# Norm statistics beside the last sums, 512-column projections and written-out layers in a two-block transformer kernel

## The reference

```
def hybrid_layer(x, ...):            # block 1, twice
    h = rmsnorm(x, norm_mix); proj = h @ w_in
    ... fox attention, compressed/selected/window attention, gates ...
    x = x + mixed @ w_out
    h = rmsnorm(x, norm_mlp)
    return x + jnp.square(jax.nn.relu(h @ w_up)) @ w_down
x = rmsnorm(x, norm_final)           # between the blocks
for i in range(2):                   # block 2
    mix = even_mixer(x, ...) if i % 2 == 0 else odd_mixer(x, ...)
    x = layer_norm(ALPHA * x + mix @ w_o[i], ln1_g[i], ln1_b[i])
    ffn = expert_choice_moe(x, ...)
    ple = sigmoid(x @ ple_gate_w[i] + ple_gate_b[i]) * (p[i] @ ple_w[i])
    x = layer_norm(ALPHA * x + ffn + ple, ln2_g[i], ln2_b[i])
# odd_mixer: q, k, v = split(x @ w_in); q = rms_norm(q per head), k = rms_norm(k per head);
# q, k = apply_rope(q), apply_rope(k); softmax(q k^T * HEAD_DIM**-0.5) v
```

## Time and profile before

| | us |
|---|---|
| median of 3 runs | 3708.51 (3707.27 to 3711.32) |
| the profiled execution itself | 3716.81 |
| its span | 3715.0 |
| mean granted clock of TensorE | 0.947 |

### The profile page before, as it was taken

One profiled execution on the slowest core, in us unless ns is written; L12 is line 12 of the kernel. 1 busy time (PEld: TensorE's weight loads), 2 busy tenths in 40 slices (PEclk: granted clock), 3 DMA queues, 4 the chain that ended last, 5 costly groups with the idle time before them and its releaser, 6 DMA issues. The chain is left out here.

```text
span 3715.0 us, 42723 instructions
## 1 busy us (share of the span) xinstructions
PE 3309.8 (89%) x17174; PEld 2279.5 (61%) x17174; DVE 1294.2 (35%) x1709; ACT 976.0 (26%) x1557; POOL 295.7 (8%) x403
## 2 busy tenths in 40 slices
PE   7999899998999999999846779999978787999996
PEld 6875687876876588777744367444437356644442
DVE  4325533333524445242344543111113654311112
ACT  4225333222324414231321431000012343100001
POOL 1004100000102300000000310000000431000000
PEclk9999999999999999999967889999998898999998
DMA  5410233333320114331300124999972101599997
GB/s 155 125 46 1 68 91 91 96 86 82 106 91 23 46 33 137 92 91 34 102 7 15 57 70 160 422 425 424 424 320 78 46 24 58 215 422 424 424 424 290
DMA packets 286517, 587.41 MB, mean 158 GB/s; under 512 B 34666, under 2 KB 228408, under 8 KB 237200
## 3 DMA queue, kind: packets, MB, share of 16 engines
q1 hardware_dynamic: 286352, 585.11, 42.3%
HBM read 581.92 MB, written 2.10 MB: 157 GB/s over the span
## 5 line engine op out<-in xcount | busy, mean ns | idle before, releaser
L2018 PE MATMUL ps<-w_ring,xe 128*64 128x512 f32 x1024 | 234.3, 600 | 6.1 <-PEq L109 5.0
L305 PE MATMUL ps<-h_hi,in_w_hi 128*128 128x512 f32 (+1 forms) x528 | 209.5, 397 | 13.2 <-DVE in_w_lo L353 8.2
L305 PE MATMUL ps<-u_hi,mlp_w_hi 128*128 128x512 f32 x512 | 201.0, 393 | 12.0 <-DVE u_lo L984 12.0
L353 DVE TENSOR_TENSOR mlp_w_lo<-w_ring,mlp_w_hi 128x2048 fp32r<-128x2048 f32 x64 | 146.7, 2292 | 175.8 <-ACT mlp_w_hi L321 175.8
L305 PE MATMUL ps<-h_lo,in_w_hi 128*128 128x512 f32 (+1 forms) x528 | 207.8, 393 | 0.0
L305 PE MATMUL ps<-h_hi,in_w_lo 128*128 128x512 f32 (+1 forms) x528 | 207.5, 393 | 0.0
L305 PE MATMUL ps<-h_hi,mlp_w_hi 128*128 128x512 f32 x512 | 199.4, 389 | 5.6 <-DVE h_lo L367 5.6
L305 PE MATMUL ps<-u_lo,mlp_w_hi 128*128 128x512 f32 x512 | 200.5, 392 | 0.0
L305 PE MATMUL ps<-u_hi,mlp_w_lo 128*128 128x512 f32 x512 | 200.2, 391 | 0.0
L305 PE MATMUL ps<-h_lo,mlp_w_hi 128*128 128x512 f32 x512 | 199.2, 389 | 0.0
L305 PE MATMUL ps<-h_hi,mlp_w_lo 128*128 128x512 f32 x512 | 199.2, 389 | 0.0
(11 more groups left out here) (512 smaller groups left out, 7046.5 us busy)
## 6 DMA issues: line engine op xcount, KB each, us to landing
w_ring<-in_w SPq DMA_DIRECT2D x192, 1024.0 KB, 12.5
ex_front<-in_w SPq DMA_DIRECT2D x96, 1024.0 KB, 13.4
ex_back<-in_w SPq DMA_DIRECT2D x96, 1024.0 KB, 13.4
w_ring<-in_w_in SPq DMA_DIRECT2D x32, 1024.0 KB, 6.6
w_ring<-in_w_up SPq DMA_DIRECT2D x32, 1024.0 KB, 5.7
w_ring<-in_w_down SPq DMA_DIRECT2D x32, 1024.0 KB, 5.6
w_ring<-in_cmp_w SPq DMA_DIRECT2D x16, 512.0 KB, 4.2
w_ring<-in_w_out SPq DMA_DIRECT2D x8, 1024.0 KB, 6.3
```

The lines of the kernel that those rows point to most:

```text
L305: mm = pe.matmul(ps[0:o.rows, k % banks, 0:o.cols], lhsT, rhs, start=(j == 0), stop=(j == len(o.mm) - 1))
L353: dve.tensor_tensor(w.lo[:, n % SPLITS, 0:used], ring.slots[:, n % RING, 0:used], w.hi[:, n % SPLITS, 0:used].bitcast(F32), ALU.subtract). ...
L2018: mm = pe.matmul(ps[rows, bank + half, :], lhsT, slot(2 * m + a)[:, kk, 512 * half:512 * half + 512], start=(k == 0), stop=(k == DC - 1))
```

## The change

- The norm lead loses its norm. `rms_beside` does it beside the last outputs of the gemm before: as soon as DVE has added token tile i's first half of columns, ACT sums its squares; after the second half, ACT sums again and takes the root, and DVE scales the row into ring slots 2 and 3. `first_rows` does the first layer's norm in a stage of its own.
- `residual_tiles` has 4 x 512-column weight tiles; outputs are pieces of 12 matmuls of 512 columns in banks 4c + i that stay open over the tiles of one column half c; only the last is added to x. The MLP's down projection takes this form too; `yT`, `unflip_add` and the fence go, and `needs` waits for the u blocks of one weight tile. With `pairwise` (w_o) the last two token tiles of the second half run whole, 24 matmuls each.
- Layers of block 1 are written out; `wy` prefetches the MLP's first two weight tiles, `mlp` those of the next layer or of `ei`.
- The norm between the blocks is part of the lead of `ei`; x itself is normed by DVE beside four outputs of `ei`.
- `ln1` goes beside `w_o`: bn_stats per half row on DVE, bn_aggr, root on ACT, two passes on DVE per token tile.
- Odd layer: gemm `oi` takes k first and runs on 4 banks; squares on ACT, sums by TensorE as 128-token by 2-head columns (`sq` stationary, 2 columns moving), k's inverse root flipped, spread and multiplied in, q's left out and given to Exp as a scale (and to the maximum by one small multiply) in `gqa`; the halves are swapped by SBUF to SBUF DMA and DVE does the rotation. Stages `on` and `ro` go.
- Names get serial numbers (left out below).

```diff
-    def down(m, n):
-        if m == 0:
-            return to(yT[:, n, :], "A")
-        return dict(v=lambda e, p, st: e.tensor_tensor(yT[:, n, :], yT[:, n, :], p, ALU.add))
-    down_tiles = [[tile(half // P, P, ..., fence=(n == 0)) for n in range(DC)] for m in range(2)]
-    gemm(nc, "mlp", ps, ring, tiles, lead=rms_flips(C, x, I["norm_mlp"][l], h, ring, ...))
-    unflip_add(nc, "da", ps, C, yT, x)
+    down_tiles = [residual_tiles(I["w_down"][l], u, half // P, added(x), m * half, lambda q, m=m: m * (ups + downs) + 4 * q + 3) for m in range(2)]
+    ends = 2 * (ups + downs)
+    tail = rms_beside(C, ring, x, ..., ends - downs // 2 - 4, ends - 4)
+    gemm(nc, "mlp", ps, ring, tiles, 2, nxt, rms_flips(C, I["norm_mlp"][l], h, ring, gain[:, :]), side=tail)
-    gemm(nc, "wy", ps, ring, y_tiles + w_out, 2)
+    tail = rms_beside(C, ring, x, lambda c, i: sgb[:, 4 * c + i, :], n_y + 4, n_y + 12)
+    gemm(nc, "wy", ps, ring, y_tiles + w_out, 2, up_of(I, l, 0)[0:2], side=tail)
-    return [tile(DC, 256, lambda slot, n=n: [(slot, W(w, DC, 256 * n, 256))],
-                 lambda w, n=n: [tm(w, actT, i, 0, 256, range(DC), **add(i, n)) for i in range(TT)]) for n in range(4)]
+    def piece(w, c, i, q, **more):
+        return out(P, 512, [m for j in range(4) for m in products(actT[:, 4 * q + j, i * P:(i + 1) * P], w[:, j, :])],
+                   bank=4 * c + i, first=(q == 0), needs=needs(q) if needs and c == 0 and i == 0 else None, **more)
+    def pieces(w, c, q):
+        if pairwise and c == 1:
+            held.append(w)
+            if q == 0:
+                return [piece(w, c, i, q, final=False) for i in range(2)]
+            rest = [out(P, 512, [...held tiles, 24 products...], bank=4 * c + i, **add(i, c)) for i in (2, 3)]
+            return [piece(w, c, i, q, **add(i, c)) for i in range(2)] + rest
+        return [piece(w, c, i, q, final=(q == quarters - 1), ...) for i in range(TT)]
+    return [tile(4, 512, ..., lambda w, c=c, q=q: pieces(w, c, q)) for c in range(2) for q in range(quarters)]
...
+def rms_beside(C, ring, x, junk, front, back):
+    def square(c, i):
+        def go(act, s):
+            act.wait_ge(s.evac_v, s.done_v[(front if c == 0 else back) + i])
+            act.activation(junk(c, i), x[:, i, 512 * c:512 * c + 512], ACT.Square, accum_out=st[:, SUMS + c, i:i + 1]).then_inc(s.n_squared, 1)
+            if c == 1:
+                act.wait_ge(s.n_squared, TT + i + 1)
+                act.wait_ge(s.n_bias, 1)
+                act.activation(st[:, STD, i:i + 1], st[:, SUMS + 1, i:i + 1], ACT.Sqrt, scale=1.0 / D, bias=st[:, BIAS, i:i + 1]).then_inc(s.n_std, 1)
+        return go
+    def scale(*tokens):
+        def go(dve, s):
+            for i in tokens:
+                dve.wait_ge(s.n_std, i + 1)
+                dve.reciprocal(C.rstd[:, i:i + 1], st[:, STD, i:i + 1]).then_inc(s.n_rstd, 1)
+                dve.wait_ge(s.n_rstd, i + 1)
+                dve.tensor_scalar(rows[:, i, :], x[:, i, :], C.rstd[:, i:i + 1], None, ALU.mult).then_inc(s.n_scaled, 1)
+        return go
+    return beside(..., {back: half, back + 2: scale(0), back + 3: scale(1), back + 4: scale(2, 3)}, nothing)
...
+def layer_norm_beside(nc, ctx, C, x, gain_dram, bias_dram, label):
+    def stat(dve, s, c, i):
+        dve.wait_ge(s.evac_v, s.done_v[(FRONT if c == 0 else BACK) + i])
+        dve.bn_stats(stats[:, i, c, :], x[:, i, 512 * c:512 * c + 512]).then_inc(s.l_stats, 1)
+    def finish(dve, s, i):
+        dve.scalar_tensor_tensor(d, d, st[:, i, 0:1], rows[:, 0, :], ALU.subtract, ALU.mult).then_inc(s.l_less, 1)
+        dve.wait_ge(s.l_std, i + 1)
+        dve.reciprocal(st[:, i, 3:4], st[:, i, 2:3]).then_inc(s.l_less, 1)
+        dve.wait_ge(s.l_less, 2 * i + 2)
+        dve.scalar_tensor_tensor(d, d, st[:, i, 3:4], rows[:, 1, :], ALU.mult, ALU.add).then_inc(s.l_done, 1)
...
# attention(): peaks and exponentials
+                    if groups[g].sharp:
+                        peak.then_inc(s.peaked, 1)
+                        dve.wait_ge(s.peaked, u + 1)
+                        peak = dve.tensor_tensor(top[:, u % 8, :], top[:, u % 8, :], groups[g].sharp(i), ALU.mult)
+                                       scale=groups[g].sharp(i)[:, a:a + 1] if groups[g].sharp else 1.0)
...
+def heads_beside(nc, ctx, ps, C, I, q, k, rq):
+    def swaps(sp, s):            # per chunk, four DMAs of 32 x 512 floats
+                for b in (0, 64):
+                    sp.dma_start(tmp[b:b + 32, c % 4, :], x[b + 32:b + 64, m, :]).then_inc(s[f"n_swap{n}"], 16)
+                    sp.dma_start(tmp[b + 32:b + 64, c % 4, :], x[b:b + 32, m, :]).then_inc(s[f"n_swap{n}"], 16)
+    def rotate(n):
+            dve.wait_ge(s[f"n_swap{n}"], 64 * len(chunks))
+            ... x * cos, tmp * sin, x + tmp on DVE for each of two chunks
+    side = beside(names, sp,
+                  {3: sum_keys(0), 4: sum_keys(2), 5: flip_keys, 6: then(spread_keys(0), sum_queries(0)), 7: spread_keys(2), 8: sum_queries(1),
+                   9: sum_queries(2), V_OUT + 1: sum_queries(3)},
+                  {2: square_keys, 4: root_keys, 5: split_hi, 7: root_queries(0), 9: root_queries(1), V_OUT: root_queries(2), V_OUT + 2: root_queries(3)},
+                  {2: tables_in, 4: invert_keys, 5: then(split_lo, rotate(0)), 6: scale_keys(0), 7: then(scale_keys(2), rotate(1)),
+                   8: then(invert_queries(0), rotate(2)), 9: then(invert_queries(1), rotate(3)), V_OUT: then(invert_queries(2), rotate(4)),
+                   V_OUT + 2: rotate(5), V_OUT + 3: invert_queries(3)},
+                  pool, {1: load_tables, 5: swaps})
...
-        with nc.Fori(0, DEPTH) as l:
-            block1_layer(nc, ps, ring, C, x, I, l)
-        norm_rows(nc, "nf", C, x, I["norm_final"], None)
+        first_rows(nc, C, x, ring)
+        for l in range(DEPTH):
+            block1_layer(nc, ps, ring, C, x, I, l, 2 if l else 0, first_tiles(I["w_in"][l + 1]) if l + 1 < DEPTH else even_tiles(I))
```

More of the change, by code:

```diff
@@ L152, in W, with out @@
     return dram[row0:row0 + kc * P, c0:c0 + n].rearrange("(k p) n -> p k n", p=P)
-def out(rows, cols, mm, a=None, v=None, behind=0, run=None):
-    return Names(rows=rows, cols=cols, mm=mm, a=a, v=v, behind=behind, run=run)
+def out(rows, cols, mm, a=None, v=None, behind=0, run=None, bank=None, first=True, final=True, needs=None):
+    return Names(rows=rows, cols=cols, mm=mm, a=a, v=v, behind=behind, run=run, bank=bank, first=first, final=final, needs=needs)
 def tile(kc, n, load, outs, fence=False, raw=False):
@@ L304, in _ @@
                                 pe.wait_ge(s.lead_done, j // 3 + 1)
-                            mm = pe.matmul(ps[0:o.rows, k % banks, 0:o.cols], lhsT, rhs, start=(j == 0), stop=(j == len(o.mm) - 1))
+                            mm = pe.matmul(ps[0:o.rows, bank[k], 0:o.cols], lhsT, rhs, start=(o.first and j == 0), stop=(o.final and j == len(o.mm) - 1))
                         mm.then_inc(s.out_done, 1)
@@ L1025, in mix_tiles, with residual_tiles @@
     return tiles, mixed_of, oT_of
[L1028 to L1036 removed]
+def residual_tiles(w, actT, chunks, add, row0=0, needs=None, pairwise=False):
+    held, quarters = [], chunks // 4
+    def piece(w, c, i, q, **more):
[6 more added lines that the diff above has]
+                return [piece(w, c, i, q, final=False) for i in range(2)]
+            rest = [out(P, 512, [m for k in range(8) for m in products(actT[:, k, i * P:(i + 1) * P], held[k // 4][:, k % 4, :])],
+                        bank=4 * c + i, **add(i, c)) for i in (2, 3)]
+            return [piece(w, c, i, q, **add(i, c)) for i in range(2)] + rest
+        return [piece(w, c, i, q, final=(q == quarters - 1), **(add(i, c) if q == quarters - 1 else {})) for i in range(TT)]
+    return [tile(4, 512, lambda slot, c=c, q=q: [(slot, W(w, 4, 512 * c, 512, row0 + 512 * q))],
+                 lambda w, c=c, q=q: pieces(w, c, q)) for c in range(2) for q in range(quarters)]
@@ new lines, in added, with add, nothing, half @@
+def added(x, alpha=None):
+    def add(i, c):
+        d = x[:, i, 512 * c:512 * c + 512]
+        if alpha is None:
+            return dict(v=lambda e, p, st: e.tensor_tensor(d, d, p, ALU.add))
+        return dict(v=lambda e, p, st: e.scalar_tensor_tensor(d, d, alpha, p, ALU.mult, ALU.add))
+    return add
+def nothing(eng, s):
+    pass
+def rms_beside(C, ring, x, junk, front, back):
+    rows, st = norm_rows_of(ring), C.norm_st
+    SUMS, BIAS, STD = 0, 2, 3
+    def square(c, i):
[7 more added lines that the diff above has]
+        return go
+    def half(dve, s):
+        dve.wait_ge(s.n_squared, TT)
+        dve.tensor_scalar(st[:, BIAS, :], st[:, SUMS, :], 1.0 / D, EPS, ALU.mult, ALU.add).then_inc(s.n_bias, 1)
+    def scale(*tokens):
[6 more added lines that the diff above has]
+        return go
+    return beside("n_squared n_bias n_std n_rstd n_scaled", nothing, {}, {**{front + i + 1: square(0, i) for i in range(TT)}, **{back + i + 1: square(1, i) for i in range(TT)}},
```

(16 more changed lines are left out.)

390 lines of the change are left out of this document (281 added, 109 removed).

## The result

The changed kernel takes 3607.62 us (median of 4 runs, 3604.87 to 3609.51) against 3707.89 us (median of 4, 3704.51 to 3711.32): ratio 0.9721, 95% interval 0.9710 to 0.9733, 100 us faster. The forecast was 3585 us in a range of 3566 to 3611. The measured value is in the range, but 23 us of the forecast gain are missing. The profiled execution has a span of 3605.1 us where the one before had 3715.0, so by profiles 109.9 us went against 123.7 forecast.

The account below looks back on a forecast made before the run. TensorE, busy 3309.8 of 3715.0 us, was taken as the bound; terms summed to -123.7, giving 3585 us from the median 3708.5. Range 3566 to 3611, with bounds of the sums (-5, +13) and attention (to +14) not all at once.

Parts of the forecast that it names:

- 512 columns: Two w_out and two w_o projections: 192 matmuls of 512 columns replace 384 of 256, -9.8 us; MLP's down projection 0.
- the fences term: MLP, between up and down: TensorE's four 3.0 us waits for the last u go, with some clock, -15.4 us.
- rival A: Odd projection: rotations waiting for swap transfers hold DVE's next split and evacuation, stalling TensorE; +21 us, 3606; chance 0.11.
- The start: First norm becomes its own stage with nothing prefetched, so layer one's first matmul comes later: +10.2 us, bounds 8 to 13.
- Gaps ahead of the MLPs: Output projection's last matmul to the MLP's first: 9.4 us instead of 12.9, -3.5 twice, -7.0 us.
- Gaps behind the MLPs: To layer two 24.7 us becomes 10.5, -14.2; to the even projection 29.3 becomes 9.8, -19.5, and its clock -2.4.
- layer norm: Behind w_o: only the last row's norm is left, 5.2 us instead of 18.5 and 18.1; -13.2 and -12.9 us.
- rival C: Matmuls of 256 columns cost nothing extra, as the skill's formula has it; 9.8 us of gain goes, 3595; chance 0.05.
- Odd layer: Two head stages of 55.2 us go beside the projection, which adds 12.9, plus 1.8: -40.5 us; its attention +1.0.
- Rivals B: Behind w_o: norm rows queue up after the last sum, 12 us more twice, 3609; chance 0.05.
- D: Shorter gaps keep the clock up through the flips and the odd layer's sums take one pass: 13 more gain, 3572; 0.08.
- E: Layer two's own code must be fetched and its matmuls wait: slower than before, 3735 at 35 ns each; chance 0.01.

Follow-up runs that it names:

- b1_w32: The kernel before with n2_tables, ahead of the MLP's split weights, made 32 bytes per partition longer: 3730.87 us, ratio 1.0053.
- a5_gain256: The changed kernel with the two small gain tables (MLP and even projection) at 256 bytes per partition in place of 32: ratio 0.9674 to the kernel before.
- m1_series: The changed kernel with places made equal, first weights loaded earlier, and an added stage of 48-matmul series alone: 512-column steps such as 0.2271, 0.2290 and 0.2331 us.
- a9_wo256: The changed kernel with w_o back in four tiles of 256 columns, the norm still row by row: 3616.30 us, ratio 0.9744 to the kernel before.
- a8_odd_back: The changed kernel with the odd layer's heads (norm and rotation stages) as in the kernel before: 3643.29 us, ratio 0.9815 to the kernel before.
- a2_all128: The changed kernel with gain tables at 128 bytes and a 64-byte pad before the odd projection's split weights: ratio 0.9722 to the kernel before.

## Why the prediction was right and where it was wrong

**The step that failed** is the last sentence under "512 columns": "The MLP's down projection has 512 columns either way: 0", and with it the fences term, which counted only the waits that go and took the matmuls' own step as given. The waits were worth 16.4 us, as forecast (15.4); the step took 20.4 back, so the MLPs came out 4.0 us longer and not 15.4 shorter. The rows priced a matmul by its shape; its step also hangs on where its two operands start. The change shrank a table ahead of the weights, and 3072 matmuls of unchanged shape lost 0.0067 us each. Shown in both directions: b1_w32 puts the loss into the kernel before (+0.53%), a5_gain256 takes it out of the changed one (-0.5%), m1_series has it with nothing else running. The diff shows the cause: a tensor ahead of the MLP's weights got another size. The trace of before held a sign of it, too. In its gate and embedding projections, where the places differ by 192 bytes, 256-column matmuls are spaced otherwise than the 0.1200 us of w_o, and not evenly. Timeline, TensorE, two outputs of the kernel before, first and last of 20 steps each (0.1133 and 0.1176 us):

```profile
2236.63 0.28 PE L305 MATMUL ps<-pl_w_hi,xT_hi 128*128 128x256 f32 x1
...
2238.89 0.28 PE L305 MATMUL ps<-pl_w_hi,xT_lo 128*128 128x256 f32 x1
...
2270.06 0.28 PE L305 MATMUL ps<-pl_w_hi,xT_lo 128*128 128x256 f32 x1
...
2272.41 0.28 PE L305 MATMUL ps<-pl_w_lo,xT_hi 128*128 128x256 f32 x1
```

**How the time still fell into the range.** It lies 3.4 us inside the upper bound of 3611. That bound was made for rival A (21 us) and for the bounds of the sums and of the attention, none of which came true; that it also held a loss in the MLP that no rival names is luck, and the unforeseen 7.8 us in the first block's attention helped.

**The start** was 8.1 instead of 10.2, at the lower bound of 8: the first matmul at 34.91 where it was at 26.85. The load was issued at 23.08, as I had it (23.6), but the first tile had landed by 29.87, and from the issue to the first sum 11.8 us passed where 13.1 were taken.

**Gaps ahead of the MLPs.** Forecast 9.4 us from the last matmul to the first. After layer one's w_out the flips start 3.51 us behind it (3.7 forecast) and the gap is 9.9: ACT's first rounding begins 4.7 us behind the start of the flips (4.2 forecast), and it and DVE's rest take 1.7 (1.4 forecast). In layer two the flips took 6.42 instead of 5.35 us, at the lower clock, and it is 10.9.

```profile
516.43 5.35 PE L281 MATMUL ps<-ident,w_ring 128*128 128x128 f32 x32 [3.51 <-PEq L119]
...
521.12 3.58 ACT L343 ACTIVATE h_hi<-ps,n_tables 128x512 fp32r<-128x512 f32 x6 [2.80 <-PE ps L281]
...
522.82 0.47 PE L320 MATMUL ps<-h_hi,mlp_w_hi 128*128 128x512 f32 x1 [1.04 <-DVE h_lo L373]
```

**Gaps behind the MLPs, 512 columns and layer norm** came within 0.3, 0.9 and 0.2 us of the forecast. Against rule and rival C: a 256-column step is 0.120 us at equal places and 0.113 to 0.120 at unequal ones, a 512-column step 0.2267 and up to 0.2333. The fixed 2.5 ns on each matmul, which the Trainium skill gives (page "TensorE: Matmul & The Clock Gate", section Back-to-back issue gap), fits neither: by it they would be 0.109 and 0.216. By that rule the gain of the four projections would have been 1.9 us, 7.9 less than the 9.8 forecast, not the 7.7 that the prediction gives. Its own steps, 0.119 and 0.225, are a little short, because a count over a stretch also takes in the matmuls that its edges cut: from start to start they were 0.1200 and 0.2267. The layer norm's 5.2 us from last matmul to first flip was met (5.20 and 5.29), with the order of the tiles as a condition, as a9_wo256 showed.

**Odd layer.** The 48 sums stand in the trace as two matmuls each, 96 in six groups of 16. In five groups they start 0.106 us apart, where 0.11 was taken, and in one at the lower clock 0.150. The projection grew by 16.3 us and not by 12.9: its granted clock was 0.94, and inside it one stretch of 7 us lay at the lower level, some 3.4 us lost. The projection of before had 6.0 us at that level at its start and this one 3.4, so the clock accounts for some 2.1 of the 3.4 us; the step of 0.2291 adds 0.6. The gap to the first product of the attention fell by 53.8, where 55.2 - 1.8 was forecast. The attention grew by 1.9, not 1.0. Net 35.6 by the traces, 35 by a8_odd_back, 39.5 forecast. Rival A did not occur.

**Not foreseen:** the first block's attention, with code unchanged, went from 153.1 to 149.2 us in both layers. At its start TensorE was at its lower clock for 3.4 us in layer one and 6.8 in layer two instead of 17. In the other kernels of this study, which don't touch it either, it lay between 147 and 153 us, so these 3.9 us can't be put down to the change. It may be part of why the profiles are 109.9 us apart and the medians 100.3 (the profiled execution of before was 9 us over its median); that was not tried.

Rivals B, D and E did not occur; layer two's matmuls are spaced as layer one's, so code fetch costs nothing that can be seen.

## What to carry to other kernels

Count where each matmul's stationary and moving tensor start, modulo 256 bytes, before and after a change: any table whose size changes ahead of them moves all that follows. What counts is where the slices start that a matmul reads: in the latent attention's query projection both tensors start at the same place, but a third of the weight slices lie 128 bytes off, and the 512-column step is 0.231 on average. For 512-column products of rounded f32 operands make the difference 0 (up to 3% of the step). For 256 columns an unequal place was cheaper by 1 to 3% in most cases here, more in some outputs, but not at 128 bytes in a2_all128; measure it. Before you price a matmul by its shape, look whether matmuls of one shape are spaced alike all over the trace. When work is moved behind the last sums row by row, check that a row's last sums take TensorE longer than the row takes the engine that follows, and order the tiles so that the last pieces are long. A stage put ahead of the first gemm should carry that gemm's first loads.
